# Two hybrid layers on one core: small f32 products of the delta solve and of linear attention, packed by chunk on opposite quarters of the array

## The reference

```
decay = exp(where(incl, gcum_i - gcum_j, -inf))
a_mat = where(strict, (kb @ k.T) * decay, 0) + eye(64)
sol = triangular_solve(a_mat, [v * beta, kb * exp(gcum)], lower, unit_diagonal)
qk = where(incl, (q @ k.T) * decay, 0)
```

```
log_a = log_sigmoid(gk_low @ w_gk_up + b_gk) / 16        # gk_low: 16 wide
b = cumsum(log_a)
attn[i, j] = sum_k q[i, k] * exp(b[i, k] - b[j, k]) * k[j, k]   for j <= i
```

## Time and profile before

| | us |
|---|---|
| Median of 3 runs | 1163.02 |
| Profiled execution, whole | 1168.86 |
| its span | 1167.1 |
| TensorE busy | 1128.1 (97%) |
| VectorE busy | 787.8 (68%) |
| ScalarE busy | 553.0 (47%) |
| mean granted TensorE clock | 0.986 of full |

### The profile page before, as it was taken

How to read it: one execution, slowest core, us unless ns; L and a number is a source line. 1 busy time by engine, 2 the same in 40 slices (tenths; PEclk the granted TensorE clock), 3 DMA queues, 4 the chain that set the end, 5 groups by cost and what they waited for, 6 DMA issues and landing times.

```text
span 1167.1 us, 16821 instructions
## 1 busy us (share of the span) xinstructions
PE 1128.1 (97%) x7102; PEld 1003.4 (86%) x7102; DVE 787.8 (68%) x948; ACT 553.0 (47%) x642; POOL 43.4 (4%) x108
## 2 busy tenths in 40 slices
PE   7989999999999999999998999999999999999996
PEld 6888897998899999998787788888889998888885
DVE  4576778555477998888587466556657876656654
ACT  6466564224445444444665354444454474444443
POOL 8000000000000000000003100000000000000000
PEclk9998999999999999999999999999989999999999
DMA  9986975538355655554554356566534435566551
GB/s 281 175 164 74 145 145 109 67 79 133 121 180 172 201 181 181 181 186 175 174 166 140 113 167 195 181 192 197 188 109 145 145 108 181 180 191 197 190 180 54
DMA packets 128509, 185.02 MB, mean 159 GB/s; under 512 B 6933, under 2 KB 104226, under 8 KB 128435
## 3 DMA queue, kind: packets, MB, share of 16 engines
q1 hardware_dynamic: 123200, 182.46, 55.4%
q10 hardware_dynamic: 4690, 1.36, 0.5%
q0 software_dynamic: 544, 0.13, 0.1%
HBM read 182.89 MB, written 1.05 MB: 158 GB/s over the span
## 4 chain that ended last, share of the span: by engine, by line
PE 85%; DVE 10%; ACT 2%; issue 2%; DMA 1%; ACTq 0%; DVEq 0%
PE ps L2021 11%; PE ps L2023 11%; PE ps L2036 11%; PE ps L1962 10%; PE ps L2001 9%; PE ps L2002 9%; PE ps L2007 8%; PE ps L1968 5%; DVE low L1313 2%; PE ps L2354 1%; DVE arena L1472 1%; PE ps L2222 1%; PE ps L2051 1%; PE ps L2228 1%; DMA arena<-in_ab_lambda 1%
## 5 line engine op out<-in xcount | busy, mean ns | idle before, releaser
L925 ACT ACTIVATE whi<-raw 128x2048 fp32r<-128x2048 f32 x170 | 324.3, 1913 | 344.1 <-PE ps L2036 160.6
L1313 DVE TENSOR_TENSOR low<-raw,whi 128x2048 fp32r<-128x2048 f32 x170 | 388.7, 2289 | 45.0 <-ACT whi L925 42.1
L2001 PE MATMUL ps<-hboth,whi 128*128 128x256 f32 x944 | 239.2, 290 | 1.5 <-ACT conv L1021 1.5
L2002 PE MATMUL ps<-hboth,whi 128*128 128x256 f32 x944 | 234.8, 286 | 0.0
L2001 PEld LDWEIGHTS ps<-hboth,whi 128*128 128x128 f32 x944 | 183.8, 195 | 6.1 <-issue 3.6
L2002 PEld LDWEIGHTS ps<-hboth,whi 128*128 128x128 f32 x944 | 183.9, 195 | 0.7 <-issue 0.2
L2021 PE MATMUL ps<-whi,ahi 128*128 128x512 f32 x416 | 164.8, 396 | 6.0 <-issue 3.6
L2023 PE MATMUL ps<-whi,alo 128*128 128x512 f32 x416 | 163.5, 393 | 0.0
L2007 PE MATMUL ps<-hboth,low 128*128 128x256 f32 x944 | 133.4, 284 | 0.3 <-DVE low L1313 0.3
L1962 PE MATMUL ps<-hboth,whi 128*128 128x512 f32 x512 | 128.1, 391 | 0.0
L2007 PEld LDWEIGHTS ps<-hboth,low 128*128 128x128 f32 x944 | 122.8, 193 | 0.5 <-DVE low L1313 0.5
(11 more groups left out here) (388 smaller groups left out, 1278.4 us busy)
## 6 DMA issues: line engine op xcount, KB each, us to landing
raw<-in_ffn_w SPq DMA_DIRECT2D x64, 1024.0 KB, 5.5
raw<-in_w_in SPq DMA_DIRECT2D x30, 1024.0 KB, 10.3
raw<-in_w_up SPq DMA_DIRECT2D x22, 1024.0 KB, 5.0
raw<-in_gla_w_in SPq DMA_DIRECT2D x12, 1024.0 KB, 5.2
raw<-in_w_down SPq DMA_DIRECT2D x11, 1024.0 KB, 4.9
raw<-in_ab_w_in SPq DMA_DIRECT2D x8, 1024.0 KB, 5.3
raw<-in_w_branch SPq DMA_DIRECT2D x6, 1024.0 KB, 5.0
raw<-in_w_o SPq DMA_DIRECT2D x4, 1024.0 KB, 4.8
```

The costliest lines, as they stand in the source:

```text
L925: act.activation(whi[:, u % SPLIT, :], raw[:, u % RAW, :], ACT.Copy).then_inc(sem("hi_done"), 1)
L1313: dve.tensor_tensor(wlo[:, u % RAW, :], raw[:, u % RAW, :], whi[:, u % SPLIT, :].bitcast(F32), ALU.subtract).then_inc(sem("lo_done"), 1)
L2001: pe.matmul(out, wh, hi[:, k0 + k, :], start=opens and k == 0, stop=False, skip_group_check=True)
L2002: pe.matmul(out, wh, lo[:, k0 + k, :], start=False, stop=False, skip_group_check=True)
```

## The change

The two chunks of a tile are no longer held in one 128x128 block matrix: chunk 0 keeps partitions 0 to 63, chunk 1 partitions 64 to 127, and both use the same 64 columns. A head's product becomes two with 64 columns, one for each chunk, which lie on opposite quarters of the array (rows and output of the same half), or, where the contraction is over 128 channels, on opposite halves of the columns. X, XT, LT, Bl, Y and DT are 128x256 and not 128x512. Packed masks (`packs`: levels, triangle, identity) are copied by GpSimd at the start. `dn_x0`'s transposes become products with the packed identity. `dn_z` does the product for X first, and `dn_y` waits for X only. `dn_sol` uses banks of its own for each tile. In linear attention levels 0 to 6 write 64-column products of all chunks into one bank, alternating between banks 6 and 7, `Cl` has two buffers, the masks collect in `near`, and ScalarE copies `near` to the diagonal of `attn` at level 7. The gate's bias becomes row 16 of `wgu`, against a row of ones in `gkT` that GpSimd writes. The orders of gates, of some units and the `steps_at` tables are new in the front, in the second attention and in linear attention.

```diff
+    fox(2, 0)
     dn(0)
-    fox(2, 0)
+    fox(2, 1)
     fox(1, 1)
-    fox(2, 1)
+    dn(5)
     dn(4)
...
-        15: [("small",), ("small_turn",)],
+        13: [("small",)],
+        15: [("small_turn",)],
...
-        24: [("fox_turn", 1), ("dn_silu",)],
-        26: [("fox_cum", 0), ("fox_cum", 1), ("dn_square",), ("dn_cum",), ("dn_unit",)],
+        23: [("fox_turn", 1)],
+        24: [("fox_cum", 0), ("dn_silu",)],
+        26: [("fox_cum", 1), ("dn_square",), ("dn_cum",), ("dn_unit",)],
...
-        48: [("dn_x0", 0), ("dn_x0", 1), ("dn_y", 0, 1), ("dn_y", 1, 1)],
-        49: [("dn_z", 0, 1), ("dn_z", 1, 1)],
-        50: [("dn_y", 0, 2), ("dn_y", 1, 2), ("dn_z", 0, 2)],
-        51: [("dn_z", 1, 2)],
-        52: [("dn_y", 0, 3)],
-        53: [("dn_y", 1, 3), ("dn_z", 0, 3), ("dn_z", 1, 3)],
-        54: [("dn_y", 0, 4)],
-        55: [("dn_y", 1, 4), ("dn_z", 0, 4), ("dn_z", 1, 4)],
-        56: [("dn_y", 0, 5), ("dn_y", 1, 5), ("dn_z", 0, 5), ("dn_z", 1, 5), ("dn_sol", 0), ("dn_sol", 1), ("dn_new", 0), ("dn_state", 0)],
+        50: [("dn_x0", 0), ("dn_x0", 1), ("dn_y", 0, 1)],
+        51: [("dn_y", 1, 1), ("dn_z", 0, 1), ("dn_z", 1, 1)],
+        52: [("dn_y", 0, 2)],
+        53: [("dn_y", 1, 2), ("dn_z", 0, 2), ("dn_z", 1, 2)],
+        54: [("dn_y", 0, 3), ("dn_y", 1, 3), ("dn_z", 0, 3), ("dn_z", 1, 3)],
+        56: [("dn_y", 0, 4)],
+        57: [("dn_y", 1, 4), ("dn_z", 0, 4), ("dn_z", 1, 4)],
+        58: [("dn_y", 0, 5), ("dn_y", 1, 5), ("dn_z", 0, 5)],
+        59: [("dn_z", 1, 5), ("dn_sol", 0)],
+        60: [("dn_sol", 1), ("dn_new", 0), ("dn_state", 0), ("dn_new", 1)],
...
-        15: [("att_norm", 1, 5), ("ab_sum", 0), ("att_turn", 1, 5), ("att_values", 1, 4), ("att_values", 1, 5), ("ab_turn", 0)],
+        15: [("att_norm", 1, 5), ("ab_sum", 0), ("att_turn", 1, 5), ("ab_turn", 0), ("att_values", 1, 4), ("att_values", 1, 5)],
...
-        6: [("gla_cum",)],
-        8: [("gla_pairs", 0), ("gla_arg", 0)],
-        9: [("gla_mul", 0), ("gla_mask", 0), ("gla_pairs", 1), ("gla_arg", 1), ("gla_mask", 1), ("gla_mul", 1)],
-        10: [("gla_arg", 2), ("gla_pairs", 2)],
...
+        7: [("gla_arg", 0)],
+        8: [("gla_pairs", 0), ("gla_mul", 0)],
+        9: [("gla_mask", 0), ("gla_arg", 1), ("gla_pairs", 1)],
+        10: [("gla_mask", 1), ("gla_mul", 1), ("gla_arg", 2)],
+        11: [("gla_pairs", 2), ("gla_mask", 2), ("gla_mul", 2), ("gla_arg", 3)],
...
+        def packed(one, half):
+            return by(one[:, half * DH * CH:(half + 1) * DH * CH], DH)
+
+        X, XT, LT, Bl = [[packed(a_, k), packed(b_, k)] for a_, b_, k in
+                         ((own_[0], tops[0], 0), (own_[1], tops[1], 0), (own_[1], tops[1], 1), (flat[0], tops[2], 0))]
+        Y = DT = [packed(flat[1], 0), packed(tops[2], 1)]
...
+        Cl = [tiles(view(3072, 1024)), tiles(view(6144, 1024))]
+        near = view(7680, 512).rearrange("p (g i) -> p g i", g=TT * GH)
...
+            for c_ in chunks:
+                then(pool.tensor_copy(trip[c_, :], tri[c_, c_]))
+                then(pool.tensor_copy(idp[c_, :], ident[c_, c_]))
+                then(pool.tensor_copy(levp[c_, :, :], lev[c_, :, c_]))
...
+            pool.memset(gkT[0:32, :], 1.0).then_inc(sem("gla_ones"), 1)
+            pool.wait_ge(sem("gla_abs"), 1)
+            pool.memset(attn[CH:P, :, 0:CH], 0.0).then_inc(sem("gla_zero"), 1)
...
-                act.activation(Y[t], by(ps[:, 7 - t, :], DH), ACT.Copy).then_inc(sem("dn_Y"), 1)
+                act.activation(Y[t], packed(ps[:, 7 - t, :], 0), ACT.Copy).then_inc(sem("dn_Y"), 1)
...
+            def gla_mask(l):
+                if l != 7:
+                    return
+                act.wait_ge(sem("gla_took"), 7)
+                for c_ in chunks:
+                    ins = act.activation(attn[c_, :, c_], near[c_, :, :], ACT.Copy)
+                ins.then_inc(sem("gla_near"), 1)
...
             def dn_pre(t):
-                dve.tensor_tensor(X[t], wide(tri64[:, :].unsqueeze(1), [DH, P]),
+                if t == 0:
+                    dve.wait_ge(sem("constants"), made["delta"])
+                dve.tensor_tensor(grows[t], wide(tri64[:, :].unsqueeze(1), [DH, P]),
-                link(dve.tensor_tensor(DT[t], by(ps[:, grow_bank[t], :], DH),
-                                       wide(gcol[:, t, :].unsqueeze(2), [DH, P]), ALU.subtract))
+                for c_ in chunks:
+                    ins = dve.tensor_tensor(DT[t][c_], by(ps[c_, grow_bank[t], :], DH)[:, :, c_],
+                                            gcol[c_, t, :].unsqueeze(2).to_broadcast([CH, DH, CH]), ALU.subtract)
+                link(ins)
...
-                if l == LEVELS - 1:
-                    dve.wait_ge(sem("dn_XBX"), 4 * (l - 1) + t + 1)
-                    own(dve.tensor_tensor(XT[t], XT[t], by(ps[:, 2 * t, :], DH), ALU.subtract), "dn_X2", 4 * (l - 1) + t + 1)
-                    return
-                dve.wait_ge(sem("dn_XBX"), 2 * n_)
-                own(dve.tensor_tensor(XT[t], XT[t], by(ps[:, 2 * t, :], DH), ALU.subtract), "dn_X2", 2 * n_ - 1)
-                own(dve.tensor_tensor(X[t], X[t], by(ps[:, 2 * t + 1, :], DH), ALU.subtract), "dn_X2", 2 * n_)
+                last = l == LEVELS - 1
+                if not last:
+                    dve.wait_ge(sem("dn_XBX"), 2 * n_ - 1)
+                    own(dve.tensor_tensor(X[t], X[t], packed(ps[:, 2 * t + 1, :], 0), ALU.subtract), "dn_X2", 2 * n_ - 1)
+                done = 4 * (l - 1) + t + 1 if last else 2 * n_
+                dve.wait_ge(sem("dn_XBX"), done)
+                own(dve.tensor_tensor(XT[t], XT[t], packed(ps[:, 2 * t, :], 0), ALU.subtract), "dn_X2", done)
...
+                got = ps[:, 6 + l % 2, :].rearrange("p (g i) -> p g i", i=CH)
+                if l == 7:
+                    own(dve.tensor_copy(attn[0:CH, :, CH:P], got[0:CH]), "gla_took", 8)
                     return
                 if l == 0:
-                    own(dve.tensor_tensor(attn, two, wide(ident[:, :].unsqueeze(1), [TT * GH, P]), ALU.mult), "gla_took", 1)
+                    own(dve.tensor_tensor(near, got, wide(idp.unsqueeze(1), [TT * GH, CH]), ALU.mult), "gla_took", 1)
                     return
-                mask = lev[:, l - 1, :].bitcast(mybir.dt.uint32)
-                own(dve.copy_predicated(attn, wide(mask.unsqueeze(1), [TT * GH, P]), two), "gla_took", l + 1)
+                mask = levp[:, l - 1, :].bitcast(mybir.dt.uint32)
+                own(dve.copy_predicated(near, wide(mask.unsqueeze(1), [TT * GH, CH]), got), "gla_took", l + 1)
...
-                else:
-                    dve.wait_ge(sem("gla_paired"), 2 * l + 2)
+                elif l > 1:
+                    dve.wait_ge(sem("gla_paired"), l)
...
-                pe.matmul(by(ps[:, beta_bank[t], :], DH), ones[:, :], XT[t], start=True, stop=True)
-                pe.matmul(by(ps[:, grow_bank[t], :], DH), ones[:, :], X[t], start=True, stop=True)\
+                for c_ in chunks:
+                    pe.matmul(packed(ps[c_, beta_bank[t], :], 0), ones[c_, 0:CH], XT[t][c_], start=True, stop=True)
...
-                        cols_ = slice(t * P, (t + 1) * P)
-                        ins = pe.matmul(ps[:, kk_banks[t][j], h * P:(h + 1) * P], dnT[:, DH + h, cols_],
-                                        dnT[:, (DH if j == 0 else 0) + h, cols_], start=True, stop=True)
+                        for c_ in chunks:
+                            cols_ = slice(t * P + c_.start, t * P + c_.stop)
+                            ins = pe.matmul(ps[c_, kk_banks[t][j], h * CH:(h + 1) * CH], dnT[:, DH + h, cols_],
+                                            dnT[:, (DH if j == 0 else 0) + h, cols_], start=True, stop=True)
...
-                    ins = pe.transpose(ps[:, 2 * t, h * P:(h + 1) * P], XT[t][:, h, :], ident[:, :])
+                    for c_ in chunks:
+                        ins = pe.matmul(ps[c_, 2 * t, h * CH:(h + 1) * CH], XT[t][c_, h, :], idp[c_, :],
+                                        start=True, stop=True)
...
                 if l > 1:
+                    pe.wait_ge(sem("dn_X2"), 2 * (n_ - 2) - 1)
+                for h in range(DH):
+                    for c_ in chunks:
+                        ins = pe.matmul(ps[c_, 7 - t, h * CH:(h + 1) * CH], Bl[t][c_, h, :], X[t][c_, h, :],
+                                        start=True, stop=True)
+                ins.then_inc(sem("dn_BX"), 1)
+
+                pe.wait_ge(sem("dn_Y"), n_)
+                if l > 1:
                     pe.wait_ge(sem("dn_X2"), 2 * (n_ - 2))
+                if l < LEVELS - 1:
+                    for h in range(DH):
+                        for c_ in chunks:
+                            ins = pe.matmul(ps[c_, 2 * t + 1, h * CH:(h + 1) * CH], XT[t][c_, h, :], Y[t][c_, h, :],
+                                            start=True, stop=True)
+                    ins.then_inc(sem("dn_XBX"), 1)
                 for h in range(DH):
```

(56 more changed lines are left out.)

155 lines of the change are left out of this document (75 added, 80 removed).

## The result

The changed kernel takes 1148.07 us (median of four runs, 1145.38 to 1150.57) against 1163.45 for the kernel before: ratio 0.9869, 95% interval 0.9854 to 0.9883. That is 15.2 us less (13.6 to 17.0). The prediction said 1143, range 1135 to 1158, faster with 0.87. The direction and the range held; the time was 5 us short of the likeliest value. The profiled execution took 1149.01 (span 1147.3), where the sum of the prediction, made in the frame of one profiled execution, had 1149.1. That these two meet within 0.1 us is partly luck: the sum booked 1.6 us for the clock and 18.2 for everything else, and some 4.6 and 15.2 came. Most of this document is about these differences.

What follows compares the result with a forecast made beforehand. TensorE, busy 97% of the span, was taken as the bound. Delta records -9.9, its waits and clock -3.6, linear attention -4.6, gate -1.7: -19.8 from 1168.86 gives 1149.1, less 5.8 to the median: 1143 us, range 1135 to 1158.

Steps and rivals of the forecast that it cites:

- The pace of packed records: Delta solve's y and z: 28 groups of 16 packed records take 0.45 us each, not 0.89; -12.3 us.
- Rival (A): All packed products: each record costs at least 0.056 us, so packing gains nothing; 1165 us, slower than before; chance 0.10.
- Changes of mode: TensorE entering or leaving a divided array: 0.33 us each; 13 in the delta stage, +4.3 us, and +0.8 within dn_sol.
- The delta stage: Delta solve: records and mode changes -9.9 us; x0 and solution waits -3.0, late Y copies +1.0, clock -1.6.
- Gate: Gate bias product: eight records of 512 columns at 0.43 us become four; -1.7 us.
- I book nothing for that: Granted clock of 0.89 at 862:871, around the gate's products of 1 and 16 rows: no gain counted.
- rival (C): Whole kernel: the clock stays at 2.4 GHz where it had fallen; another 6 us, 1137 us; chance 0.12.
- Linear attention: Linear attention's levels: levels 0 to 6 save 4.0 us, level 7 saves 0.6, level 8 unchanged; -4.6 us.
- the projection half and product 8 between cover them: Before gla_values: TensorE work hides ScalarE's two level 7 copies, 0.6 us each; uncovered they cost 1.2 us.
- rival (B): Nine solve islands and nine levels: shorter groups no longer cover ScalarE's and VectorE's hand-overs; 8 us lost, 1151; chance 0.17.
- Orders at 0: Reordered front slots and second attention: no net effect, 0 us with 3 us to either side.
- From 1149.1 to 1143.3: Whole run: profiled-frame sum less 5.8 us, the distance of the earlier profiled execution (1168.86) above its median (1163.02).

Runs made afterwards that it cites:

- those 47 others: Timed executions of the unchanged kernel before, beside the experiments: 1161.4 us at mean clock 0.993, 1164.3 at 0.991, 1167.4 at 0.987; the line falls 1.07 us per 0.001.

## Why the prediction was right, and where it was not

- **The pace of packed records** was the main term (y and z, -12.3) and held: 0.47 a group against 0.45. The exchange of the loops shows that it is the running side by side. Rival (A) is refuted.
- **Changes of mode** at 0.33 held: counted as in the earlier trace rows, from the last record ahead to the second one behind less two ordinary gaps, each of the seven levels takes 1.27 to 1.28 us against the forecast 1.23, and 32 records at the measured pace (2 x 0.47) leave 0.33 to 0.34 of it. A solve group alone between projections leaves the same (0.80 less 0.47).
- **The delta stage**, -9.9 for records and -2.0 for waits without the clock, is 11.9; 12.4 was measured with the gate's row (14.1 less 1.7 for the clock), and some 13 at equal clock in the run with the solve alone. The reason for the x0 wait's end was half wrong: the packing did it, most likely by its smaller VectorE operations, and not the slot.
- **Gate**: -1.7 forecast for the records, 1.7 in the trace (against before, its first record stands 12.03 us earlier and its last 13.75). "I book nothing for that" of the clock is the first step that failed: it was worth some 3.5 us in the median and 3.0 in the traces, nearly twice the records. It was the part of rival (C) that came.
- **Linear attention**: -4.6 forecast; from the gate's last record to the values' first, 6.2 us went (69.20 to 63.00), 3.0 of them by the clock, as with the gate's row alone. The 3.2 left are 1.4 short, and that is the wait ahead of the values (1.6 to 1.8): "the projection half and product 8 between cover them" failed, since ScalarE had a weight split and the values' copies queued ahead. With the copies on VectorE the stretch is 4.5 us shorter than with the gate's row alone (61.72 against 66.20), the forecast's 4.6. Here rival (B) was right, once and not nine times.
- **Orders at 0**: the six traces with the new head order reach dn_tok 1.9 to 4.5 us late, the three with both halves and the old one 5.6 to 6.4, and the others 0 to 1.8 early. In four of the six the loss is 1.9 to 2.9; in the changed trace the clock fell behind the wait at 33 us as well (32.4 to 39.3), up to 3.4 of the 4.5. Late loads are what the traces show; their cause is open. No step of mine had it. It cancels most of what the packed levels bring: the kernel without them is within 1 us.
- **From 1149.1 to 1143.3** is the step that made the miss of 5 us. I took 5.8 off because the profiled execution of before lay that much above its median, as if that distance stayed. It was the clock: the profiled execution ran at 0.986, and the line through those 47 others puts 1169.4 at that clock. The changed one was profiled at 0.990, beside its own median clock of 0.9915, and 0.9 us above its median. Of the 19.85 us between the two profiled executions, 4.6 (0.004 x 1149) is clock; the rest, 15.2, is what the medians show. The sum should have been made at equal clock: its own terms without the clock are 18.2, and the excess of 3 is, as an estimate, the head (1.1 in this trace without its clock, 1.9 to 2.9 in four others) and the values' wait (1.4).

## What to carry to other kernels

Put products that use opposite parts of TensorE's array near each other in its queue; a mixed order halves their time, a sorted one gives most of that back, and each change of mode costs as much as three records at full width (0.33 us). Compare profiled executions only after setting their clocks equal, since 0.004 of mean clock was 4.6 us here, more than most single edits. Ask of every small load which queue stands still until it lands: 32 KB held up two engines for 8 to 9 us. And time the parts of a large change separately: here the smallest, four records, came with a third of the gain, and the packed levels with little that the head did not lose again.

## What the hardware showed

- Two f32 records on opposite quarters start 6 to 7 ns apart and each pair takes 58 ns at 64 columns; on one quarter, a record takes the same 58 ns. Matmuls on another quarter overtake earlier ones by a few records (L2271 starting at 211.12, the last record of L2259 at 211.28).
- The granted clock fell behind a product of one row and one of 16 rows (0.91 over 840 to 880) and not behind one of 17 rows with half as many records. TensorE was busy 39.58 and 39.57 of 40 us, so the busy time does not tell the two apart.
- Two kernels that issue the same transfers moved 141 and 308 GB/s at 20 to 24 us, and the reader of 32 KB loads issued at 28.5 and 29.8 us was held until 55.0, where the kernel before had no wait for it at 43.4. Why is open.
